# Seven block products in both gated MLPs, with another order of the products

## The reference

```python
# first block
h = rmsnorm(x, ffn_norm_g[l])
up = causal_depthwise_conv(h @ w_up[l], conv_w[l], conv_b[l])   # 3 taps along the sequence
a, bgate = jnp.split(up, [D_FF], axis=-1)
x = x + (jax.nn.silu(a) * bgate) @ w_down[l]
...
# third block
gate, up = jnp.split(h @ w_gate_up, 2, axis=-1)
ffn = (jax.nn.silu(gate) * up) @ w_down
```

## Time and profile before

| | |
|---|---|
| median of 3 runs | 3164.26 us (3163.53 to 3165.51) |
| the profiled execution, device time | 3165.08 us |
| its span, first to last instruction | 3163.8 us |
| MLP of the first block, tiles 1 to 21 and ten downs | 504.76 to 1179.6 us |
| MLP of the third block, tiles 1 to 21 and all downs | 2483.73 to 3125.7 us |

### The profile page before, as it was taken

How to read it: one execution, slowest core, us unless ns; L and a number is a source line. 1 busy time by engine, 2 the same in 40 slices (tenths; PEclk the granted TensorE clock), 3 DMA queues, 4 the chain that set the end, 5 groups by cost and what they waited for, 6 DMA issues and landing times.

```text
span 3163.8 us, 35007 instructions
## 1 busy us (share of the span) xinstructions
PE 2986.1 (94%) x14470; PEld 2321.6 (73%) x14470; DVE 1800.1 (57%) x2551; ACT 1139.5 (36%) x1680; POOL 2.2 (0%) x6
## 2 busy tenths in 40 slices
PE   8999799999999998999998989999888899999997
PEld 6787577888888876777775757665566788888885
DVE  5542336444554547666783463667664866666666
ACT  4223423222222224344445444555642522222223
POOL 0000000000000000000000000000000000000000
PEclk9999999999999998999999999999989999999999
DMA  4211011111111111111010101000001111111111
GB/s 150 72 59 37 30 49 45 47 44 50 51 50 47 47 47 40 34 40 39 28 34 21 40 27 37 24 21 28 21 25 36 34 47 54 60 47 54 60 47 67
DMA packets 48828, 141.69 MB, mean 45 GB/s; under 512 B 12790, under 2 KB 16670, under 8 KB 48542
## 3 DMA queue, kind: packets, MB, share of 16 engines
q1 hardware_dynamic: 48670, 139.45, 14.2%
HBM read 135.16 MB, written 9.77 MB: 46 GB/s over the span
## 4 chain that ended last, share of the span: by engine, by line
PE 84%; DVE 6%; ACT 6%; issue 3%; DMA 0%; SPq 0%; DVEq 0%; ACTq 0%
PE psum L509 37%; PE psum L756 13%; PE psum L989 10%; PE psum L796 8%; PE psum L543 5%; PE psum L565 2%; PE psum L896 2%; PE psum L554 1%; PE psum L1071 1%; PE psum L1098 1%; PE psum L560 1%; PE psum L916 1%; PE psum L611 1%; ACT sb_left L1778 1%; DVE residual L1949 1%
## 5 line engine op out<-in xcount | busy, mean ns | idle before, releaser
L509 PE MATMUL psum<-h_hi,w_hi 128*128 128x512 f32 x1376 | 428.0, 392 | 8.3 <-DVE ret_q L2105 3.2
L509 PE MATMUL psum<-h_hi,w_lo 128*128 128x512 f32 x1376 | 424.0, 389 | 0.0
L509 PE MATMUL psum<-h_lo,w_hi 128*128 128x512 f32 x1376 | 423.9, 389 | 0.0
L1934 DVE TENSOR_TENSOR w_lo<-w_raw,w_hi 128x1024 fp32r<-128x1024 f32 x164 | 200.3, 1221 | 218.5 <-ACT w_hi L1183 218.2
L509 PEld LDWEIGHTS psum<-h_hi,w_hi 128*128 128x128 f32 x1376 | 256.9, 188 | 65.8 <-issue 10.7
L509 PEld LDWEIGHTS psum<-h_lo,w_hi 128*128 128x128 f32 x1376 | 258.3, 188 | 54.0
L509 PEld LDWEIGHTS psum<-h_hi,w_lo 128*128 128x128 f32 x1376 | 258.3, 188 | 53.9
L2227 DVE TENSOR_TENSOR residual<-residual,psum 128x1024 f32<-128x1024 f32 x176 | 214.5, 1219 | 141.8 <-PE psum L796 70.3
L1183 ACT ACTIVATE w_hi<-w_raw 128x1024 fp32r<-128x1024 f32 x164 | 172.5, 1052 | 237.8 <-PE psum L509 188.3
L989 PE MATMUL psum<-h_hi,w_hi 128*128 128x512 f32 x576 | 211.5, 446 | 4.9 <-ACT cln_rstd L1195 2.0
L989 PE MATMUL psum<-h_hi,w_lo 128*128 128x512 f32 x576 | 203.9, 414 | 0.0
(11 more groups left out here) (348 smaller groups left out, 5245.8 us busy)
## 6 DMA issues: line engine op xcount, KB each, us to landing
w_raw<-in_weights SPq DMA_DIRECT2D x228, 512.0 KB, 3.6
residual<-in_x_t SPq DMA_DIRECT2D x8, 512.0 KB, 9.5
out_t<-residual SPq DMA_DIRECT2D x8, 512.0 KB, 3.0
rel_copies<-rel_rows SPq DMA_DIRECT2D x8, 480.0 KB, 5.9
na_bias<-rel_copies SPq DMA_DIRECT2D x8, 240.0 KB, 4.2
band_copies<-band_rows SPq DMA_DIRECT2D x8, 192.0 KB, 6.3
ret_rotary<-in_rotary SPq DMA_DIRECT2D x1, 1024.0 KB, 12.5
swa_bias<-band_copies SPq DMA_DIRECT2D x4, 256.0 KB, 2.8
```

The source lines that it names most:

```text
L509: ins = self.pe.matmul(out[:, s], w[:, k, at:at + P], src(k, low)[:, s], start=(k == 0 and part == 0), stop=(k == n_k - 1 and part == 2))
L1934: self.dve.tensor_tensor(self.m.w_lo[:, n % 2, :], self.m.raw[:, n % 2, :], self.m.w_hi[:, n % 2, :].bitcast(F32), ALU.subtract).then_inc( ...
```

## The change

`mlp` and `strassen` become one function `mlp(plan, norm)`, used for both MLPs with `PLAN1` and `PLAN3`. In both, hidden tiles 0 and 1 are computed plainly (tile 1 into banks 4 to 7) and tiles 2 to 21 with seven products. The first block's MLP so goes from 22 plain tiles to 2 and 20 by seven; the third's from 1 plain and 21 by seven to 2 and 20. The products are reordered, the weight sums are made in place from other halves, and for the first block the convolution's taps are taken out of the combined product: the taps of the gate in two halves (`taps_a`, `taps_a2`, with two columns carried from the first half in `gbuf`), those of the up part from SBUF (`linear`). There are still two raw weight buffers and four half-tile weight buffers.

```diff
 class Plan:
-    G1, S2, S3, S1, G2, U2, S4 = range(7)
+    G1, S2, S1, G2, S3, S4, U2 = range(7)
...
-        self.stages = [("up", 1)]
+        self.stages = []
...
-PLAN3 = Plan(MLP3, "mlp3")
+PLAN1, PLAN3 = Plan(MLP1, "mlp1"), Plan(MLP3, "mlp3")
...
-        self.mlp(MLP1, "n2", True)
+        self.mlp(PLAN1, "n2")
...
-        self.strassen(PLAN3, "l2")
+        self.mlp(PLAN3, "l2")
...
+    def mlp(self, plan, norm):
...
+        for i in range(2):
+            t = self.tile
+            q.wait_ge(*on("w_lo", t))
+            out = self.take(("proj", t), 4 + 2 * i, 2, read[i](1))
+            self.gemm(out, KD, *self.weights(t), 0, self.h).then_inc(*self.to("proj", t))
+            self.tile += 1
         for kind, i in plan.stages:
             if kind == "up":
                 self.seven(plan, i)
...
-        bank = (0, 1, 2, 3, 0, 2, 3)
-        emptied = (("act_c11" + name, c), ("dve_u2" + name, c), ("dve_c21" + name, c), ("dve_c12" + name, c))
-        read = {4: ("act_s1" + name, c), 5: ("dve_u3" + name, c), 6: ("dve_c22" + name, c)}
+        bank = (0, 1, 3, 0, 2, 3, 2)
+        c11_read = ("dve_carry", c) if plan is PLAN1 else ("act_c11" + name, c)
+        emptied = {0: c11_read, 1: ("dve_u2" + name, c), 2: ("dve_c12" + name, c), 4: ("dve_c21" + name, c)}
+        read = {3: ("act_s1" + name, c), 5: ("dve_u4" + name, c), 6: ("dve_c22" + name, c)}
```

ScalarE's part for the first block (`conv_step`), new:

```diff
+        if j == 0:
+            q.wait_ge(*on("ms_mlp1", c, 0))
...
+                q.wait_ge(*on("dve_tap_b", c - 1, 2))
+            self.act.activation(m.us, m.place["ms_mlp1", c, 0], ACT.Copy).then_inc(*to("act_s1mlp1", c))
+            if c > 2 and c % 2 == 0:
+                self.hidden_high(plan, c - 1)
...
+        elif j == 5:
+            q.wait_ge(*on("dve_c12mlp1", c))
+            self.tap(m.ta[:, HALF:S], m.gate2, c).then_inc(*to("act_tap_a", c, 1))
+        elif j == 6:
+            q.wait_ge(*on("dve_c21mlp1", c))
+            q.wait_ge(*on("dve_hid_lomlp1", c - 1))
+            self.tap(m.tp[:], m.cb[:], c + DFF // P).then_inc(*to("act_tap_b", c))
+            self.conv_silu(c, 1, 2)
```

VectorE's part for the first block, new:

```diff
+    def taps_a2(self, c):
+        m = self.m
+        self.after("dve_c12mlp1", c)
+        self.tap("a", 1, m.ta[:, HALF:S], m.gbuf[:, 1:1 + HALF], c, (c, 1, 1), ("act_tap_a", c, 1), ("dve_carry", c))
+        self.tap("a", 2, m.ta[:, HALF:S], m.gbuf[:, 0:HALF], c, (c, 1, 2), ("dve_tap_a", c, 1, 1))
...
+    def linear(self, c):
+        m, channel = self.m, c + DFF // P
+        self.tap("b", 1, m.tp[:, 1:S], m.cb[:, 0:S - 1], channel, (c, 1), ("act_tap_b", c))
+        self.tap("b", 2, m.tp[:, 2:S], m.cb[:, 0:S - 2], channel, (c, 2), ("dve_tap_b", c, 1))
+        self.gated_tile(c)
```

VectorE's loop over blocks, where n-1 is the block just finished:

```diff
+            done = plan.last_up(n - 1)
+            if done is not None:
+                self.linear(done)
...
+            if ahead:
+                self.block_sums(plan, n + 2)
+            if kind == "up":
+                self.products(plan, c, j)
+            else:
...
+                    self.add_down(c, half, o)
```

More of the change, by code:

```diff
@@ L683, in mean_after_mix @@
         self.column_mean("mean1024", self.m.n_acc, ("pe_n2_mean",), ("act_n2_rstd", 1))
[L685 to L715, removed]
+    def mlp(self, plan, norm):
         m, q, on, name = self.m, self.q, self.on, plan.name
+        read = ((lambda c: ("dve_tap_a", c, 2), lambda c: ("dve_tap_b", c, 2)) if plan is PLAN1 else
+                (lambda c: ("act_gate" + name, c), lambda c: ("dve_m" + name, c)))
         self.n_acc += self.n_acc % 2
-        self.project_pair(lambda k: (f"act_{norm}_hi", k), lambda k: (f"dve_{norm}_lo", k), ("act_gate" + name, 0), ("dve_m" + name, 0))
+        self.project_pair(lambda k: (f"act_{norm}_hi", k), lambda k: (f"dve_{norm}_lo", k), read[0](0), read[1](0))
+        for i in range(2):
[4 more added lines that the diff above has]
+            self.tile += 1
         for kind, i in plan.stages:
@@ L755, in seven @@
                 for part, (w, x) in enumerate(((w_hi, high), (w_lo, high), (w_hi, low))):
-                    ins = self.pe.matmul(out[bank[j]], w[:, k, :], x(k), start=(j < 4 and k == 0 and part == 0),
+                    ins = self.pe.matmul(out[bank[j]], w[:, k, :], x(k), start=(j in emptied and k == 0 and part == 0),
                                          stop=(k == 3 and part == 2), skip_group_check=True)
@@ L1394, in norm4, with tap_a @@
+    def tap_a(self, c):
+        self.q.wait_ge(*self.on("ms_mlp1", c, 3))
+        self.q.wait_ge(*self.on("dve_mmlp1", c - 1))
+        self.tap(self.m.ta[:, 0:HALF], self.m.place["ms_mlp1", c, 0], c).then_inc(*self.to("act_tap_a", c, 0))
     def norm4(self):
@@ new lines, in product @@
+        def product(c):
+            q.wait_ge(*on("act_gatemlp3", c))
+            q.wait_ge(*on("proj", plan.b[c]))
+            if c:
+                self.after("dve_hid_lomlp3", c - 1)
+            else:
+                self.after("dve_t_lomlp3", 3, 2)
+            dve.tensor_tensor(m.tp[:], m.ta[:], m.place["proj", plan.b[c]], ALU.mult).then_inc(*to("dve_mmlp3", c))
+        sums(0)
+        self.split_up_to(plan.base + 2)
+        self.input_low(plan, 0, 1, 0, 2)
+        sums(1)
+        self.split_up_to(plan.base + 3)
@@ L2694, in mlp3 @@
+        self.input_low(plan, 1, 1, 0, 2)
+        for k in range(2, 4):
+            sums(k)
+            self.input_low(plan, k, 1, 0, 2)
         self.block_sums(plan, 1)
@@ L2732, in mlp3 @@
                 self.block_low(plan, n + 2)
-            if kind == "up" and j == 0 and c > 1 and c % 2 == 0:
+            if (kind, c, j) == ("up", 2, 0):
+                for k in range(4):
+                    self.input_low(plan, k, 3)
+            elif (kind, c, j) == ("up", 2, 1):
+                product(1)
+            elif (kind, c, j) == ("up", 2, 2):
+                self.hidden("mlp3", 1)
+            elif kind == "up" and j == 0 and c % 2 == 0:
                 self.hidden("mlp3", c - 1)
```

548 lines of the change are left out of this document (316 added, 232 removed).

## The result

| | device time, median (range, runs) | span of the profiled execution |
|---|---|---|
| before | 3164.89 us (3163.53 to 3165.76, 4) | 3163.8 us |
| after | 3137.24 us (3133.22 to 3138.44, 4) | 3137.1 us |

The changed kernel takes 0.9911 of the time, 95% interval 0.9894 to 0.9928: 27.7 us less, or 0.9%. The forecast was 3127.0 us, 37.9 less than that median of before, with a range from 3108 to 3150. The sign and the range held; 10 us of the expected gain did not come.

The account below looks back on a forecast made before the run. TensorE was taken to bound both MLPs, so fewer matmuls save time if VectorE keeps up. Terms summed to -37.3 us on the 3163.8 us span, 3126.5, giving a forecast of 3127.0 us, range 3108 to 3150.

Parts of the forecast that it names:

- matmuls: First block's MLP: tiles 2 to 21 go from plain to seven products, 20 x 2.72 us saved, -54.4 us.
- head of the third MLP: Start of the third block's MLP: plain tile 1 hides VectorE's input sums, so TensorE's 10.24 us wait goes; -10.0 us.
- head of the first MLP: Start of the first block's MLP: TensorE's 0.99 us wait for taps goes, as tile 1 has its own banks; -1.0 us.
- first group: First MLP, tile 2 and down 0: VectorE late, stalls of 1.7 and 4.2 us; +6.0 us, between 0 and 9.
- nine down stages: First MLP, after even tiles: taps and gated product delay the down's first addition, TensorE stalls 2.29 us each; +20.6 us.
- odd turns: First MLP, from an odd tile to the next even one: 0.8 us of cover at the tightest, so no cost; 0.
- end of the first MLP: After the last up product: first addition at about 10.3 us, norm's sums end 36.1 after it, 39.6 before; -3.5 us.
- clock: First MLP: three of ten new waits drop TensorE's clock to half, 1.5 us each; +5 us, ends 0 and 15.
- signs that the forecast named for the trace: Waits of 2.0 to 2.6 us in nine downs, longer in the first; none at L743 in odd tiles; 19.04 us up stages.
- late chain: VectorE's chain after a tile runs 0.8 us later than walked, through handoffs, with more clock drops: 3146 us; chance 0.25.
- slower rival: Taps with both operands in SBUF take far longer than from PSUM; if doubled 3213 us, slower than before; chance 0.05.
- full cover: First MLP: taps don't delay the down stages' additions, so 20.6, 4.2 and 5 us of cost go: 3097 us; chance 0.07.

Follow-up runs that it names:

- third part alone: Kernel after with the first block's MLP put back as in the kernel before, only the third block's MLP changed: 3154.55 us, ratio 0.9972 to the kernel before.
- short-wait version: Kernel after with only each inner down stage's first addition ahead of the taps and gated product in the first block's MLP: 3111.75 us, ratio 0.9833 to the kernel before.

## Why the prediction was right, and what was off

| step | forecast, us | from the traces, us |
|---|---|---|
| matmuls | -54.4 | -54.4 |
| head of the third MLP | -10.0 | -10.0 |
| head of the first MLP | -1.0 | -2.3 |
| first group: tile 2 and down 0, without the clock | +6.0 | +5.3 |
| nine down stages, without the clock | +20.6 | +26.3 |
| odd turns | 0 | 0 |
| end of the first MLP | -3.5 | -3.2 |
| clock | +5 | +12.9 |
| elsewhere | 0 | -1.0 |
| sum on the span | -37.3 | -26.7 (the terms give -26.4) |

The signs that the forecast named for the trace came with two exceptions: three of the nine steady waits are longer than 2.0 to 2.6 us, and the first down's wait is not longer than the others but 2.37 us too. The measured 3137.24 lies at the upper end of the 3118 to 3137 that were given to the forecast itself (its terms' own ends, 0 to 9 and 0 to 15, add up to 3116 to 3140), and is nearer to the late chain's 3146 than to 3127.0. The mechanism was the forecast's; that the range held owes much to its width.

**Matmuls and price.** Every pair of tiles by seven products in the first MLP has 38.08 us between its starts, as forecast from the earlier trace rows.

**Head of the third MLP.** Pair to first down stage: 74.79 us before, 64.78 after. The walk of VectorE's queue had ended 1.1 us ahead of the need, and it was enough. The third part alone (9.3 us) confirms the size in time.

**Head of the first MLP.** The 0.99 wait is gone. The other 1.3 is the pair of tiles ahead of it, shorter by how its half-clock stretch fell (24.72 us before without the wait, 23.43 now), which the change does not touch: a gain by luck.

**First group.** Forecast 1.7 for c22 and 4.2 for down 0; read 2.35 of wait for c22 (2.65 of excess without the clock) and 2.67 of excess in down 0. The sum was right to 0.7 and its split was not: when c22 is later, the down stage begins later too, and part of VectorE's lateness is paid there. Moving c22 showed that the two are one sum.

**The even turn, mis-sized by 5.7 us.** The mechanism is what the forecast walked. The wait of 2.37 is its 2.29, but the stage is 2.67 longer. Nine times 0.38 is 3.4; that 0.3 us of excess comes on top of a wait was seen in the short-wait version too (0.85 and 1.16) and with S4 ahead of S3 (0.78 and 1.07), and I had left it out. The other 2.3 are three loads that land late, a term the forecast did not have: it took the low part of the down tile's weight as ready. (The forecast's own figures, 7.69 and 5.44, are 2.25 apart; the 2.29 that it multiplied has a handoff of 0.04 more.)

**Taps from SBUF.** The one price that the trace of before did not have. VectorE's groups from 560 to 1160 us in the kernel after (busy, mean ns, idle): whole taps from SBUF, half taps from PSUM, half taps from SBUF.

```profile
L2239 DVE SCALAR_TENSOR_TENSOR mlp_tp<-mlp_cb,vectors,mlp_tp 128x1023 f32<-128x1023 f32 (+1 forms) x36 | 46.1, 1281 | 0.6
L2239 DVE SCALAR_TENSOR_TENSOR mlp_ta<-psum,vectors,mlp_ta 128x511 f32<-128x511 f32 (+1 forms) x37 | 27.7, 748 | 17.1 <-ACT mlp_ta L1320 16.4
L2239 DVE SCALAR_TENSOR_TENSOR mlp_ta<-mlp_gate,vectors,mlp_ta 128x512 f32<-128x512 f32 x36 | 27.0, 749 | 0.6
```

1281 ns from SBUF against 1282 from PSUM before, 749 against 748 for a half: taken as 1.28 and 0.75, and the slower rival, which needed taps 1.4 times as dear, had no ground.

By the cycle table of the Trainium skill (VectorE: DVE Perf Modes, section on the TRN2 errata) the SBUF forms would be 62 cycles shorter, 65 ns at 0.96 GHz as an estimate. These rows show no difference, so it was right not to use it.

**Odd turns.** No wait ahead of L743 after tile 2. The cover was thin: the low part for the fifth product ends at 600.81 and is needed at 601.35, 0.54 us where I had 0.8. One operation more on the chain, 1.07 us, then cost 0.79 in most pairs.

**Clock, mis-sized by 8 us: the largest miss.** The price per drop was right (forecast 1.5, read 1.6); the count was not. I took three of ten, from one wait with a drop and one without in the earlier trace rows. It fell behind seven of the nine steady waits and in tile 2, and not in down 0. Two downs with the same wait, on TensorE's timeline:

```profile
682.40 0.73 PE L783 MATMUL psum<-mlp_act_hi,w_hi 128*128 128x512 f32 x2 [2.37 <-DVE residual L2353]
...
810.70 0.73 PE L783 MATMUL psum<-mlp_act_hi,w_hi 128*128 128x512 f32 x2 [2.37 <-DVE residual L2353]
```

And the windows right behind them, columns as before:

```profile
682.50:686.00 3.50, 3.50 (x10) 2.79 (x11) 1.58 (x2) 0.00 (x0) 0.00 (x0) 0.60 0.24 43
810.80:814.20 3.40, 3.40 (x15) 2.83 (x16) 2.02 (x3) 0.00 (x0) 0.00 (x0) 1.00 0.24 35
```

After one the granted clock is 0.60 and ten matmuls are done in the window (1.2 GHz for most of it), after the other 1.00 and fifteen (2.4 GHz). What stood ahead is the same in both: some 62 us of matmuls without a gap, then 2.37 us of wait. With waits so near each other there was no ground in two rows for a share of three in ten; taking the one dropped of the two as a half would have given some eight us instead of five.

**End of the first MLP.** From the last up product to the first matmul behind the norm 53.6 us before, 50.42 now: 3.2 less, where 3.5 was forecast. The close agreement is in part luck. VectorE's part, to the end of the norm's sums, took some 36.9 us and not the 36.1 forecast, 2.7 less than the 39.6 before; its first addition starts some 12 us behind the last product and not 10.3. The other 0.5 is in the norm behind it (14.98 before, 14.51 now).

**Rivals.** The full cover at 3097 did not happen, for the reason given against it, and became the version with the additions between the taps: 3099.66. The late chain at 3146 has the right kind of cost, more drops of the clock, but not its cause: in six of the nine downs the chain ran 0.2 us later, not 0.8, the odd turns stayed free, and the 0.7 to 0.8 more in the other three came from late loads and not from handoffs. At 1.3 us more than walked it gives 3166.12, so the slower rival, though it had no ground in the taps' price, stood nearer than it was put.

## What to carry to other kernels

When an edit gives VectorE more work in a stage where TensorE never waited, do not ask only whether the sum fits: find the first operation on which TensorE's next buffer depends and count what now stands ahead of it in the queue. Moving two additions forward, with nothing else changed, was worth 37.6 us here, more than the change itself. And price a new wait at more than its length: here 0.3 us to get going again, and 1.6 us more (up to 2.7 with waits of 3.4 us) if the clock falls behind it, for which a range of "none" to "all" is more honest than a share.

## What the runs showed of the hardware

- Waits of the same length, behind the same work, may or may not be followed by a half clock. Of nine steady waits of 2.37 us with small loads five were, four weren't; in the kernel after it was four of six, and three of three of 3.08 to 3.18 us. Nine waits of 0.85 us never were. In the order of time neither of the first two shows a regular pattern, but with S4 ahead of S3, where the nine waits are 2.37 us too, every other one was, five of nine. So neither the length of the wait nor the work ahead of it decides alone; what does stays open.
- A drop cost 1.6 us in the kernel after (4.26 against 2.67 of excess), behind waits of 2.37 and of 3.1 us alike. It is not a fixed price: with one operation more on the chain the clock fell behind all nine waits, eight of 3.4 us and one of 4.05, and it cost 1.4 to 1.6 us in five downs and 2.6 to 2.7 in four, every other one. Two neighbouring downs of that version, from the windows (columns as before; granted clock 0.94 and 0.88), with waits of the same 3.44 us:

```profile
746.00:773.00 27.00, 23.56 (x97) 19.08 (x96) 19.53 (x21) 5.25 (x8) 0.00 (x0) 0.94 0.12 40
812.00:840.10 28.10, 24.66 (x97) 19.84 (x96) 19.53 (x21) 5.19 (x7) 0.00 (x0) 0.88 0.13 38
```

- The load of a 512 KB weight tile lands after 3.7 us in the median of this stretch, and after 3.2 to 5.5 us in all. One that is late costs time only where the chain waits for it, in three of nine down tiles here, at 4.75 to 4.85; why these three are late stays open. With an eighth of a down tile's bytes ScalarE's waits for loads fall from 46.1 to 28.5 us.
